# Order of two steps in GpSimd's loop over expert entries: finished rows first, then the requests for the entry four ahead

## The reference, cut to what matters

```
_, idx = top_k(masked, 8)                  # 8 of 64 experts for each token
for each expert e, in blocks of its tokens:
    xb  = h[tokens of e]                   # rows of 1024 float32
    hid = silu(xb @ w1[e]) * (xb @ w3[e])  # 1024 -> 256
    y[tokens of e] += (hid @ w2[e]) * weight
```

## Time and profile before

| | |
|---|---|
| time, median of 3 runs | 2477.69 us (2475.12 to 2478.83) |
| the profiled execution's own time | 2461.14 us |
| its span | 2459.4 us |
| PE busy | 2400.4 us, 98% |
| DVE, ACT, POOL busy | 1179.6, 482.6, 616.1 us |
| DMA packets of q1 and q0, share of the 16 engines | 35.8% and 19.5% over the whole span |

### The profile page before, as it was taken

One profiled execution on the slowest core, in us unless ns is written; L12 is line 12 of the kernel. 1 busy time (PEld: TensorE's weight loads), 2 busy tenths in 40 slices (PEclk: granted clock), 3 DMA queues, 4 the chain that ended last, 5 costly groups with the idle time before them and its releaser, 6 DMA issues.

```text
span 2459.4 us, 32897 instructions
## 1 busy us (share of the span) xinstructions
PE 2400.4 (98%) x8544; PEld 1175.8 (48%) x8545; DVE 1179.6 (48%) x2744; ACT 482.6 (20%) x892; POOL 616.1 (25%) x628
## 2 busy tenths in 40 slices
PE   6999999999999999999999999999999999999997
PEld 3444444555544556665444455444444444444443
DVE  3377212666755666657335676443333333343332
ACT  3311000444432133333211112200000000000000
POOL 0000000000022100000211143555555545455441
PEclk9999999999999999999999999999999999999998
DMA  8132333443362333212433412599899999999995
GB/s 260 42 73 48 81 77 115 110 136 108 119 181 65 82 81 95 90 44 86 133 110 113 128 61 105 196 306 300 287 303 332 333 325 340 314 359 364 327 317 132
DMA packets 121190, 435.26 MB, mean 177 GB/s; under 512 B 21004, under 2 KB 23260, under 8 KB 95376
## 3 DMA queue, kind: packets, MB, share of 16 engines
q1 hardware_dynamic: 78208, 306.91, 35.8%
q0 software_dynamic: 42896, 127.25, 19.5%
HBM read 366.44 MB, written 71.70 MB: 178 GB/s over the span
## 4 chain that ended last, share of the span: by engine, by line
PE 89%; DVE 6%; DMA 1%; issue 1%; SPq 1%; ACT 1%; POOL 0%; DVEq 0%; POOLq 0%; ACTq 0%
PE psum L980 22%; PE psum L1462 17%; PE psum L1529 9%; PE psum L1065 8%; PE psum L1311 7%; PE psum L1467 5%; PE psum L1328 3%; PE psum L1268 2%; PE psum L1535 2%; PE psum L1372 2%; PE psum L1136 2%; PE psum L1146 2%; PE psum L1155 2%; PE psum L1395 1%; DMA mem<-in_ada_w 1%
## 5 line engine op out<-in xcount | busy, mean ns | idle before, releaser
L980 PE MATMUL psum<-mem 128*128 128x512 f32 x1536 | 690.2, 595 | 1.0 <-ACT mem L1656 1.0
L1462 PE MATMUL psum<-mem 128*128 x1008 | 449.9, 594 | 1.5 <-DVE mem L2673 1.0
L980 PEld LDWEIGHTS psum<-mem 128*128 128x128 f32 x1536 | 279.9, 191 | 294.4 <-issue 291.4
L785 POOL DMA_INDIRECT mem<-h_d,idx x287 | 293.7, 1023 | 354.6 <-DVE idx L2774 257.0
L1462 PEld LDWEIGHTS psum<-mem 128*128 128x128 f32 x1008 | 186.6, 190 | 229.6 <-issue 229.6
L2752 DVE TENSOR_TENSOR mem<-mem,psum 128x256 f32<-128x256 f32 x93 | 39.1, 421 | 419.0 <-ACT mem L1941 417.4
L1529 PE MATMUL psum<-mem 128*128 128x512 f32 x504 | 228.0, 599 | 1.0 <-issue 0.6
L1065 PE MATMUL psum<-mem 128*128 128x512 f32 x448 | 192.8, 592 | 0.0
L790 POOL DMA_INDIRECT out_x<-mem,put x93 | 140.5, 1510 | 99.0 <-issue 73.3
L1311 PE MATMUL psum<-mem 128*128 128x512 f32 x384 | 165.0, 592 | 0.0
L1529 PEld LDWEIGHTS psum<-mem 128*128 128x128 f32 x504 | 93.0, 190 | 124.6 <-issue 124.6
(11 more groups left out here) (421 smaller groups left out, 2488.4 us busy)
## 6 DMA issues: line engine op xcount, KB each, us to landing
mem<-in_exp_w SPq DMA_DIRECT2D x201, 1024.0 KB, 8.8
mem<-in_w_in SPq DMA_DIRECT2D x16, 2048.0 KB, 14.2
proj_d<-mem SPq DMA_DIRECT2D x104, 256.0 KB, 2.0
mem<-in_ada_w POOLq DMA_DIRECT2D x16, 1024.0 KB, 6.3
mem<-proj_d POOLq DMA_DIRECT2D x56, 256.0 KB, 3.0
mem<-proj_d POOLq DMA_DIRECT2D x20, 512.0 KB, 5.7
mem<-in_ada_w SPq DMA_DIRECT2D x4, 2048.0 KB, 23.0
mem<-in_w_branch SPq DMA_DIRECT2D x3, 2048.0 KB, 8.0
```

Of the source, the lines that this page charges most:

```text
L785: g.indirect_dma_start(x[:, 2 * P * n:2 * P * (n + 1)], None, h2_q, bass.IndirectOffsetOnAxis(ap=idx[:, p, j, n:n + 1], axis=0), bounds_ch ...
L980: mm = t.matmul(bank(unit_bank(u)), l, r, start=(k == 0), stop=(k == KD - 1))
L1462: return t.matmul(bank(up_banks[j][r]), xgT[r][:, k, P * j:P * (j + 1)], up_piece(h, r, k), start=(k == 0), stop=(k == KD - 1))
```

## The change

In each iteration, GpSimd now does `add_rows` for entry i-1 first and `fetch_ahead` for entry i+4 after it. The counts, waits, buffers and all other engines' programs stay as they are.

```
@@ pool_pair
     for p in range(2):
         i = 2 * it + p
-        fetch_ahead(i, p)
         with pool.If(pool.snap(n_last) > 0):
             add_rows(pool.snap(n_last), 1 - p, pool.snap(i + 2))
         pool.nop()
+        fetch_ahead(i, p)
         pool.reg_mov(n_last, tokens(pool, i))
```

## The result

| | changed kernel | kernel before |
|---|---|---|
| time, median | 2507.09 us (2499.72 to 2511.76, 4 runs) | 2477.59 us (2475.12 to 2478.83, 4 runs) |
| profiled execution: time, span, clock | 2507.46, 2505.8 us, 0.99 | 2461.14, 2459.4 us, 0.996 |

The ratio is 1.0118 (95% interval 1.0092 to 1.0143): 29.5 us slower. Forecast was 2478.7, "no change", up to 2494.

A forecast was written before the change was run, and what follows sets the result against it. PE's own matmuls were taken as the bound. Adds 0 us, nearly all requests 0 us and 1 us for single large entries, put on the 2477.7 us median, gave 2478.7 us; own range 2474 to 2483, 8 in 10 reaching to 2494.

The forecast's parts named there:

- PE's matmuls set the time, DMA engines full: Entry loop, 1840 to 2300 us: PE busy 458.96 of 460.00 us, so it bounds the kernel; DMA share 0.98.
- Adds forward, worth nothing: GpSimd's adds, moved before the requests, start earlier; PE waits for none of them: 0 us.
- run 2 us ahead: GpSimd's adds start 2 us earlier than now; 0 if their chain is full everywhere, 7.6 at most for entry 44.
- Requests of large entries back by 8.8 us, turning 0.8 to 4.6 late, hidden in 5.6: Entry 49's requests start 8.8 us later, DVE's turning follows late; PE's 5.6 us slack before entry 47's down products hides it.
- the smaller lateness: Requests no longer behind a two-tile add land in 4.4 to 7.0 us: turning 0.8 to 3.4 us late.
- The sum, +1 us: Adds 0 us, nearly all requests 0 us, 1 us allowed for single large entries whose lateness goes past 5.6 us.
- The chain of adds: Rival, chance 0.24: requests waiting for the preceding add in add_rows close a loop that becomes the bound; 14 us slower, 2492.
- The tail: Last entries keep their order of steps, so the final wait of 5.59 us for a two-tile add stays: 0 us.
- who waits for that: After the late turning, DVE writes idx and weighs entry 46; PE needs that at entry 47's down products, slack 5.6 us.

The follow-up runs named there:

- same_after: The changed kernel, unchanged, run again beside the kernel before on the first chip: 2462.16 us, ratio 1.0009.
- light_before: The kernel before with half of w3 and half of w2 left unloaded, on the third chip: ratio 1.0004.
- same_before: The kernel before, unchanged, run again on the first chip for a second trace: 2460.34 us, ratio 1.000.
- wait_only: The kernel before, with GpSimd also waiting in front of the requests until the adds of the entry before have landed: 2628.32 us, ratio 1.068.
- before_2: The kernel before, unchanged, on the second chip: 2473.44 us, ratio 0.9997.
- after: The changed kernel as first measured and profiled: median 2507.09 us, ratio 1.0118; profiled execution 2507.46 us.
- after_2: The changed kernel, unchanged, on the second chip: 2503.79 us, ratio 1.0108.
- after_3: The changed kernel, unchanged, on the fourth chip: 2503.43 us, ratio 1.0127.
- light_after_3: The changed kernel with half of w3 and half of w2 left unloaded, on the fourth chip: 2493.08 us, ratio 1.008.
- short_before_3: The kernel before with adds that move 16 rows each (output incomplete), on the fourth chip: 2479.61 us, ratio 1.0022.
- short_after_3: The changed kernel with adds that move 16 rows each (output incomplete), on the fourth chip: 2460.08 us, ratio 0.9947.

## Why the prediction was wrong, step by step

**PE's matmuls set the time, DMA engines full.** Right where no hand-off is late (from 1840 to 2300 same_after has PE busy for 458.09 of 460 us). That the DMA engines are full did not matter there: light_before, with a third of the weights left unloaded, has ratio 1.0004.

**Adds forward, worth nothing.** Right in the price: same_after adds nothing to PE's waits but 0.7 us at L1535. Wrong in the size: the adds were taken to run 2 us ahead. Against PE, whose down products of entry 47 come 1.9 us later in this trace (2218.94 for 2217.00), entry 44's add is 0.25 us ahead (2197.37 for 2195.68).

**Requests of large entries back by 8.8 us, turning 0.8 to 4.6 late, hidden in 5.6.** The outcome is right, in part by luck. With the same 1.9 us taken off, the first request of entry 49 moved back by 10.6 us, not 8.8, since the adds were not ahead; it is now 11.3 us after `idx`, against 0.9 us before. The last request's rows are used 2212.37 - 2205.76 = 6.6 us after its start, not 8.2. The two errors cancel: the turning is 4.7 us late against 4.6 forecast, and 1.3 us of the 5.6 are left. At 2253.6 nothing is left and PE waits 0.66 us, which is the 1 us that the sum allowed. The 6.6 us are in line with the smaller lateness which the Trainium skill's rule on ring order ("DMA: Bandwidth & Descriptors", section "Queues, rings and completion order") would give; one entry doesn't test the rule, and the sum is the same without it.

**The sum, +1 us.** Right where nothing else happened: over the entry loop same_after stands 1.1 us behind same_before, ratio 1.0009.

**The chain of adds.** It did not close in the changed kernel; in wait_only, where the requests stand between the landing and the next add, the loop is 6.8% slower.

**The tail.** Unchanged: the gap of 1.5 us before the last down products is in all traces.

**The step that failed** is the last of the sum: "that execution is 16.6 us under the median of the runs, of which its rows tell nothing, so I put the same difference onto the median". The 16.6 us were the sign that the measured runs held something that the profiled one did not, and that it was not a constant. The runs showed what stands there: on some chips PE's signal to ACT is late when requests have just been issued, 12.5 us of PE waits in the order of before and 30.4 us in the changed one. The change moves exactly those requests. In the prediction's terms the list of "who waits for that" ended at DVE's turning; the requests' issue itself, beside PE's transposes, was in no case, and the hand-off had only half a microsecond of cover.

Where the 29.5 us went, by the loop's steps in the traces: from the first entry's transposes to the last the changed kernel takes 31.6 us more than before_2, a trace of the kernel before from another chip with late hand-offs. 23.7 us are more idle time of PE (40.6 against 16.9 us after 1590 us, gaps over 0.15 us). Some 8 us are slower matmuls behind the long gaps. The gap of 8.82 us ends at 1877.60. The granted clock of 1870 to 1880 us is 0.58, most of it at 1.2 GHz, and that of 1880 to 1890 is 0.90 (columns as in the earlier trace rows):

```profile
1870.00:1880.00 10.00, 2.40 (x3) 1.17 (x4) 0.42 (x1) 1.05 (x3) 4.64 (x4) 0.58 0.92 266
1880.00:1890.00 10.00, 10.00 (x22) 4.29 (x21) 5.59 (x9) 0.00 (x0) 2.39 (x2) 0.90 0.37 72
```

The sixteen down products behind the gap take 9.27 us; in same_after, without a gap and at a granted clock of 1.00, they take 7.13. The 1 us gaps of the order before draw no such loss: in before_2 the granted clock is 1.00 from 1600 to 2200 us, and a triple grows by its gap alone (39.29 us with a gap of 1.13, against 38.20 in same_before). This is why few long waits cost more than many short ones.

**Left open:** why a hand-off is late at all. Part of it may be the weights' queue: in before_2, after, after_2, after_3, light_after_3 and short_before_3, 51 hand-offs have two or more requests before them and q1 starting again, after a pause of over 1 us, 0.4 to 2 us before the transposes end, and 34 of these are late; of the 119 with the requests alone, 11 are. But of the 17 such hand-offs of same_before and same_after none is late, and the other five traces of the chips with late hand-offs don't bear it out: 8 of 18 with both are late, and 27 of 128 with the requests alone. Whether it is GpSimd's making of descriptors, the packets, something outside the core, or what makes the slow stretches, no run here separates; nor why only some chips show it.

## What to carry to other kernels

When the profiled execution is outside the spread of the timed runs, the difference is a term with a cause of its own: ask what it could be before adding it as a constant, and widen the range towards it. Look not only at what waits for a moved DMA but at the short hand-offs between engines beside its issue, and at how much work covers each: here half a microsecond. And measure an order on more than one chip before judging it: this one costs 0.1% on the first chip, and 1.1 to 1.3% on the second, on the fourth and in the first result.

## What the runs showed of the hardware

- A hand-off PE to ACT of 0.04 us became 0.8 to 9.4 us on some chips while GpSimd issued indirect DMAs, and in 0 of 241 cases when none of the row requests started 0.3 to 4.4 us before. PE's semaphore updates were then recorded late and together (1876.53, 1876.58 and 1876.70 for matmuls that end from 1867.0 to 1868.8), those of DMAs were not held up.
- On the same chips branch and register instructions, of DVE, GpSimd and SP above all, took about 0.70 us in stretches of 2 to 15 us, some 50 to 100 us in a trace (about 20 in short_after_3, nearly all before 1640 us); 61 of 83 late hand-offs lie beside such an instruction, and 61 of 575 others.
- After single gaps of 2.7 to 8.9 us the next matmuls ran part of their time at the lower clock, 1.0 to 3.1 us lost at each; after the gaps of about 1 us in before_2, none.
- Adds that move 16 rows instead of up to 128 change the time by only 0.13 to 0.16% on a quiet chip (0.9984, 0.9985 and 0.9987): the full adds cost the loop nearly nothing there.
